# Sample attention of a one-core decoder step: key tiles moved between the compression units, value fills between the later ones, masks applied after the scores

## What is computed

```python
def compress(rows, pe, w1, w2):            # 32-token blocks at stride 16
    ...
    for j in range(n_part):
        pre = pre + u[:, j, j:j + n_blk]
    return jnp.einsum('bngh,hd->bngd', jax.nn.silu(pre), w2)

def cmp_branch(q, q_pos, kc_rows, vc_rows, W):
    kc = rmsnorm(compress(kc_rows, ...), W['k_norm'])
    vc = compress(vc_rows, ...)
    ...
    return attend_shared(q, q_pos, kc, vc, e, mask, W['rel_bias'])   # also gives p_cmp

def select_blocks(p_cmp, q_pos, n_sel, k_top):   # the 16 best blocks of 64 tokens
    imp = jnp.sum(p_cmp, axis=3)
    ...
    _, idx = lax.top_k(score, k_top)
    return idx
```

## Time and profile before

| what | us |
|---|---|
| median of 3 runs | 1774.26 (1773.98 to 1776.72) |
| the profiled execution, its own time | 1760.02 |
| its span, first to last instruction | 1758.2 |
| PE busy in it | 1669.6 (95%) |
| DVE busy | 1148.0 (65%) |
| ACT busy | 762.8 (43%) |
| granted TensorE clock, mean | 0.98 of 2.4 GHz |

### The profile page before, as it was taken

The page is one execution under the profiler, slowest core; times in us unless marked ns, Lnnn a source line. Parts: engine busy times, 40 slices in busy tenths (PEclk is TensorE's granted clock), DMA queues, the critical chain, the costliest instruction groups (busy, mean ns, idle before and its releaser), DMA issues. The chain is left out here.

```text
span 1758.2 us, 32849 instructions
## 1 busy us (share of the span) xinstructions
PE 1669.6 (95%) x11957; PEld 1434.0 (82%) x11957; DVE 1148.0 (65%) x2529; ACT 762.8 (43%) x1585; POOL 432.1 (25%) x548
## 2 busy tenths in 40 slices
PE   5999999799998989998987998999999999999999
PEld 5999999689887666655655877999999999977887
DVE  6632247666766555556464368887778887687885
ACT  6322453677774235456443234322322332365342
POOL 1321110666775543334352001000000000040000
PEclk9999999799999989999998999999999999999999
DMA  5533211120101247547593232322222332593343
GB/s 162 99 107 108 53 43 26 25 50 21 25 16 29 65 143 272 192 142 272 173 398 136 73 97 65 116 91 97 90 90 94 107 112 84 176 381 96 94 120 108
DMA packets 158858, 204.24 MB, mean 116 GB/s; under 512 B 55110, under 2 KB 109423, under 8 KB 158674
## 3 DMA queue, kind: packets, MB, share of 16 engines
q1 hardware_dynamic: 136058, 121.66, 23.2%
q0 software_dynamic: 22368, 80.46, 12.9%
q10 hardware_dynamic: 312, 0.52, 0.1%
HBM read 164.69 MB, written 37.90 MB: 115 GB/s over the span
## 5 line engine op out<-in xcount | busy, mean ns | idle before, releaser
L2977 PE MATMUL banks<-u_sum,w_sum 128*128 128x264 f32 x2904 | 358.4, 285 | 3.4 <-DVE w_sum L3008 3.4
L2977 PEld LDWEIGHTS banks<-u_sum,w_sum 128*128 128x128 f32 x2904 | 355.7, 189 | 4.1 <-DVE w_sum L3008 4.0
L470 PE MATMUL banks<-u_parts_mix,w_in_parts 128*128 128x352 f32 x1440 | 243.5, 326 | 4.4 <-DVE u_parts_mix L838 4.4
L470 PEld LDWEIGHTS banks<-u_parts_mix,w_in_parts 128*128 128x128 f32 x1440 | 230.7, 189 | 7.8 <-DVE u_parts_mix L838 4.8
L1982 PE MATMUL banks<-turned,cmp_w 128*128 128x512 f32 x256 | 133.4, 603 | 4.7 <-DVE turned L2109 3.0
L2107 ACT ACTIVATE turned<-banks 128x512 f32<-128x512 f32 (+1 forms) x136 | 78.7, 587 | 125.8 <-PE banks L1970 125.5
L3316 PE MATMUL banks<-wd_hi,gd_hi 128*128 128x512 f32 x308 | 120.2, 390 | 1.4 <-DVE gd_lo L3347 1.0
L3316 PE MATMUL banks<-wd_lo,gd_hi 128*128 128x512 f32 x308 | 120.0, 390 | 0.0
L3316 PE MATMUL banks<-wd_hi,gd_lo 128*128 128x512 f32 x308 | 119.9, 389 | 0.0
L1970 PEld LDWEIGHTS banks<-consts,rows_grouped 128*128 128x128 f32 x512 | 64.7, 144 | 66.7 <-issue 57.2
L3204 POOL DMA_DIRECT2D rest_whole<-g_rest x1 | 0.6, 594 | 466.3 <-issue 466.3
(11 more groups left out here) (459 smaller groups left out, 3340.1 us busy)
## 6 DMA issues: line engine op xcount, KB each, us to landing
gd_whole<-g_sums SPq DMA_DIRECT2D x77, 256.0 KB, 2.7
g_sums<-silu_gate SPq DMA_DIRECT2D x55, 256.0 KB, 2.1
w_gate_raw<-in_w_gate SPq DMA_DIRECT2D x11, 1024.0 KB, 5.4
w_up_raw<-in_w_up SPq DMA_DIRECT2D x11, 1024.0 KB, 5.4
w<-in_w_down POOLq DMA_DIRECT2D x33, 256.0 KB, 18.4
w_in_raw<-in_w_in SPq DMA_DIRECT2D x29, 256.0 KB, 3.4
g_sums<-s SPq DMA_DIRECT2D x22, 256.0 KB, 2.3
x_tile<-in_x_prompt SPq DMA_DIRECT2D x8, 512.0 KB, 4.1
```

The lines of the kernel that those rows point to most:

```text
L470: mm = nc.tensor.matmul(bank[:, 0:PIECE], w[:, pb, :], u[:, pa, k, tokens(p)], start=(k == 0 and (pa, pb) == TERMS[0]), stop=(k == KT - 1 ...
L2977: mm = nc.tensor.matmul(bank(tg, i), wp[side, p][:, a, k, :], m.u[tg, i, b][:, k, :], start=(k == 0 and (a, b) == TERMS[0]), stop=(k == kh ...
```

## The change

`sample_order` is rewritten. In the first half each of units 0 to 7 is followed by one key tile of half 0, and the window follows tile 7; `kc` of half 0 stands inside unit 8. Then units 9 and 10. The ten value fills of half 0 stand one behind each half of units 11 to 14 (eight), two behind unit 14. Tiles 0 and 1 of half 1 stand inside unit 15, tiles 2 to 4 behind it, then `kc`, tiles 5 to 7, window, values. The mask of half 0 can't be there when its tiles are scored, so all eight tiles of each half are copied raw by ACT, and DVE masks and reduces them later, in four pieces of 1024 columns (`mask_max`), in four steps that follow each other. The scores of half 0 go to banks 6 and 7. `sample_chunks` follows the new order. The queries are placed (16 small copies) after unit 0 instead of unit 3. ACT copies half of each key tile's fills in both halves.

```diff
@@ sample_order
-    for u in range(9):
-        fills += comp(u)
-    fills += comp(9, range(6)) + kc(0) + comp(9, range(6, 8)) + comp(10) + keys(0) + win(0)
-    for u in range(11, 16):
-        fills += comp(u)
-    return fills + weights(0) + keys(1, range(1)) + kc(1) + keys(1, range(1, 8)) + win(1) + weights(1)
+    for m in range(4):
+        fills += comp(2 * m) + keys(0, [2 * m]) + comp(2 * m + 1) + keys(0, [2 * m + 1])
+    fills += win(0) + comp(8, range(2)) + kc(0) + comp(8, range(2, 8)) + comp(9) + comp(10)
+    for i in range(8):
+        fills += comp(11 + i // 2, range(4 * (i % 2), 4 * (i % 2) + 4)) + weights(0)[i:i + 1]
+    fills += weights(0)[8:] + comp(15, range(4)) + keys(1, range(2)) + comp(15, range(4, 8))
+    return fills + keys(1, range(2, 5)) + kc(1) + keys(1, range(5, 8)) + win(1) + weights(1)
@@ sample_chunks
+    for m in range(4):
+        chunks += comp(2 * m) + four("keys", 0, m) + comp(2 * m + 1)
+    chunks += comp(8) + comp(9) + comp(10)
+    for m in range(4):
+        chunks += comp(11 + m, [0]) + four("values", 0, m) + comp(11 + m, [1])
...
@@ the vector engine
-                def mask_first(hb):
-                    dve.wait_ge(s.raw_taken, 4 * hb + 4)
-                    dve.wait_ge(s.masked, hb + 1)
...
+                def mask_max(hb, e):
+                    dve.wait_ge(s.raw_taken, 8 * hb + 2 * e + 2)
+                    dve.wait_ge(s.masked, hb + 1)
+                    half = e // 2
+                    part = w.ss[:, DS + 1024 * e:DS + 1024 * (e + 1)]
+                    if half:
+                        near = part.rearrange("p (s n) -> p s n", s=8)[:, :, 120:128]
...
+                        chain(nc.vector.tensor_tensor(near, near, recent, ALU.add))
+                    v = part.rearrange("p (s j x) -> p s j x", s=8, x=4)
+                    chain(nc.vector.tensor_tensor(
+                        v, v, w.mask[:, 32 * half:32 * half + 32].unsqueeze(1).unsqueeze(3).broadcast_to([P, 8, 32, 4]),
+                        ALU.add))
+                    chain(nc.vector.tensor_reduce(w.pm[:, e:e + 1], part, AX.X, ALU.max))
...
+                        for e in range(4):
+                            if since == ((28, 29, 30, 31), (26, 27, 28, 29))[hb][e]:
+                                mask_max(hb, e)
@@ the scalar engine
-                        for j in range(4):
+                        for j in range(8):
                             if f == at["keys", hb, j, 3] + 2:
                                 raw_scores(hb, j)
-                        for e, later in enumerate(((6, 9, 12, 15), (3, 4, 5, 7))[hb]):
-                            if f == at["keys", hb, 7, 3] + later:
+                        for e, since in enumerate(((32, 33, 34, 35), (30, 31, 32, 34))[hb]):
+                            if f == END[hb] + since:
                                 scores_exp(hb, e)
```

More of the change, by code:

```diff
@@ L1799, in sample_order, with key_bank @@
     fills = []
-    for u in range(9):
-        fills += comp(u)
-    fills += comp(9, range(6)) + kc(0) + comp(9, range(6, 8)) + comp(10) + keys(0) + win(0)
-    for u in range(11, 16):
-        fills += comp(u)
-    return fills + weights(0) + keys(1, range(1)) + kc(1) + keys(1, range(1, 8)) + win(1) + weights(1)
-def sample_chunks():
-    comp = lambda us: [("comp", u, sh, h) for u in us for sh in range(2) for h in range(2)]
-    four = lambda kind, hb: [(kind, hb, h, sh, b) for h in range(2) for sh in range(2) for b in range(B4)]
-    return (comp(range(11)) + four("keys", 0) + comp(range(11, 16)) + four("values", 0) + four("keys", 1) +
-            four("values", 1))
+    for m in range(4):
[5 more added lines that the diff above has]
+    return fills + keys(1, range(2, 5)) + kc(1) + keys(1, range(5, 8)) + win(1) + weights(1)
+def sample_chunks():
+    comp = lambda u, halves=range(2): [("comp", u, sh, h) for sh in halves for h in range(2)]
+    four = lambda kind, hb, m: [(kind, hb, m // 2, m % 2, b) for b in range(B4)]
+    chunks = []
+    for m in range(4):
[3 more added lines that the diff above has]
+        chunks += comp(11 + m, [0]) + four("values", 0, m) + comp(11 + m, [1])
+    chunks += comp(15, [0]) + four("keys", 1, 0) + comp(15, [1])
+    for kind, first in (("keys", 1), ("values", 0)):
+        for m in range(first, 4):
+            chunks += four(kind, 1, m)
+    return chunks
+def key_bank(hb, j):
+    return j % 2 if hb and j >= 2 else 6 + j % 2
 def ring_slot(m, n):
@@ L1851, in by_act @@
         if kind == "keys":
-            return order[f][3] % 2 == 1 or (order[f][2] >= 4 and order[f][3] == 2)
+            return order[f][3] % 2 == 1
         if kind == "comp":
@@ L2022, in score @@
                         copied(pe, f - 3 + b)
-                    if j < 2:
-                        pe.wait_ge(s.added, 2 * (10 + j) if hb == 0 else 32)
-                    elif j < 6:
-                        pe.wait_ge(s.raw_taken, 4 * hb + j - 1)
-                    else:
-                        pe.wait_ge(s.s_taken, 4 * hb + j - 5)
+                    if hb == 0 and j == 0:
+                        pe.wait_ge(s.q_placed, 1)
+                    if hb and j < 2:
+                        pe.wait_ge(s.o_ready, 1)
+                    elif hb and j < 4:
+                        pe.wait_ge(s.added, 32)
+                    elif j >= 2:
+                        pe.wait_ge(s.raw_taken, 8 * hb + j - 1)
                     for b in range(B4):
-                        mm = nc.tensor.matmul(m.bank[(j + 1) % 2][32 * b:32 * b + 32, :], w.q[:, hb, b, :],
+                        mm = nc.tensor.matmul(m.bank[key_bank(hb, j)][32 * b:32 * b + 32, :], w.q[:, hb, b, :],
                                               w.fill[:, (f - 3 + b) % SLOTS, :], start=True, stop=True)
@@ L2054, in weigh @@
                     copied(pe, f)
-                    if hb and i == 0:
-                        pe.wait_ge(s.o_ready, 1)
+                    if i == 0:
+                        if hb:
+                            pe.wait_ge(s.o_ready, 1)
+                        else:
+                            pe.wait_ge(s.w_taken, 1)
                     if i < 8 and i % 2 == 0:
@@ L2089, in _ @@
                         project(LAST[f - 4])
-                    if f - 22 in END:
-                        importance(END.index(f - 22))
+                    for hb in range(2):
+                        if f == END[hb] + (22, 20)[hb]:
+                            importance(hb)
                     turn(f + 3)
@@ L2165, in raw_scores @@
                         weights_turned(act, 7)
[L2166 removed]
+                    nc.scalar.activation(w.ss[:, DS + j * 512:DS + (j + 1) * 512], m.bank[key_bank(hb, j)][:, :],
                                          ACT.Copy).then_inc(s.raw_taken, 1)
@@ L2265, in compressed_max @@
                                             negate=True).then_inc(s.c_ready, 1)
-                    chain(nc.vector.tensor_reduce(w.pm[:, 5:6], w.ss[:, 0:DS], AX.X, ALU.max))
+                    chain(nc.vector.tensor_reduce(w.pm[:, 4:5], w.ss[:, 0:DS], AX.X, ALU.max))
                 def compressed_weights(hb):
@@ L2329, in take_window @@
                         weights_turned(dve, 9)
-                    nc.vector.tensor_copy(w.sw[:, 0:WIN], m.bank[1][:, :]).then_inc(s.w_taken, 1)
+                    nc.vector.tensor_copy(w.sw[:, 0:WIN], m.bank[key_bank(hb, 7)][:, :]).then_inc(s.w_taken, 1)
                     dve.wait_ge(s.w_taken, hb + 1)
```

74 lines of the change are left out of this document (21 added, 53 removed).

## The result

The changed kernel takes 1819.45 us (median of 4 runs, 1817.32 to 1820.69) where the kernel before took 1774.12 beside it: 2.5% slower, ratio 1.0253 (95% interval 1.0235 to 1.027). The forecast was 1815, slower. The profiled execution took 1818.66 us, 58.6 more than the one before was forecast from. Outside the stage nothing moved: 813.6 us follow its last output, 813.8 before. The stage itself ran from 645.5 to 1003.2, 357.7 us instead of 298.9, where some 340 had been forecast.

What follows compares the result with a forecast made beforehand. PE was taken to bound the stage, so only its waits counted: 58.2 us comes, 17.6 goes, +40.6 on the profiled 1760.0. With 14.2 from profile to median that made 1815, range 1797 to 1833.

Steps and rivals of the forecast that it cites:

- (a): Key tiles behind units 0 to 7 and 15: PE waits 1.19 us for a late DVE copy, nine times, 10.7.
- (b): Normalisation ahead of `kc` in both halves: PE waits 5.3 and 4.4 us, 13.3 with two low stretches.
- (f): Query copies, first half's gathers and raw copies come at no cost; gathers 0 to 6 us if slow, 0 taken.
- (c): Half 0's mask pieces in unit 10: waits of 5.1 us, 6.9 with a low stretch, plus 2.0 for exponentials: 8.9.
- (d): Ring of gathers, units 12 to 14: slots free late, wait 3.4 us plus low stretch 1.8, three times: 15.6.
- (e): Half 1's mask pieces behind tile 7: first weights 12.3 us after its score, 7.9 more, 9.7 with a low stretch.
- The 4.17 stays: Second half's values: PE's 4.17 us wait for the last value gathers remains, since they are issued as before.
- Clock: After longer idle times PE runs slowly for a stretch, each costing 1.8 us.
- the 3.63: PE's 3.63 us wait for half 0's last value gathers, forecast to go; a block at full speed, 1.08, followed it.
- PE's lead hides it: Rival: PE turning three fills ahead covers late copies, so (a), (c) and (d) vanish: 1768 us, chance 0.06.
- Slower, and more: Rival: first half's gathers land late, (f) and ring waits at 6 each, regroupings hold tiles' copies: 1830 us, chance 0.13.
- Slower, but less: Rival: the clock doesn't fall after the new waits, or only after some: 1802 us, chance 0.16.

Runs made afterwards that it cites:

- the pair from one chip: Kernel before and changed kernel, both unchanged, run and traced in one set on one chip (kind A): 1775.75 and 1816.75 us.
- e_regroup_early: On top of `e_keys_last`, two regroupings of each unit after a first-half key tile moved ahead of the tile: 1798.49 us, 40.5 above before (kind B).
- e_six: Changed kernel with gathers reordered, normalisation earlier, masks spread, then adds, Silu and projection one step later: 1778.38 us, 3.3 above before (kind A).
- kind B: Sets of runs in which the kernel before takes 1758 us; the one recorded chip is 11.
- kind A: Sets of runs in which the kernel before takes 1774 to 1775 us; the recorded chip is 12.
- e_keys_last: Changed kernel with the second unit's four chunks gathered ahead of the key tiles' four in the first half's pairs: 1806.63 us, 33.1 above before (kind A).
- e_after_again: The changed kernel, unchanged, run again beside the kernel before (kind A): 1816.75 us against 1775.75, ratio 1.0239.
- e_no_mask_add: Changed kernel without the addition of the block mask to the raw scores in both halves: 1786.44 us, 28.4 above before (kind B).

## Why the prediction was right

The median came out 4.5 us above the forecast, inside the range. Its steps, with the sizes in the pair from one chip unless another trace is named:

- **(a)** Nine waits at tiles forecast at 10.7: 10.5 (eight in the first half, one in unit 15). `e_regroup_early` shows that it isn't the regroupings, and in `e_six` moving the two adds by one fill (with Silu and projection) was enough to end seven of them; the shift alone was never moved.
- **(b)** Waits of 5.3 and 4.4 forecast: 5.8 (1.31, 0.88, 3.62) and 3.4 here, 4.45 and 3.42 in kind B. In kind A too it is 4.45 alone where the bursts of gathers are shorter (`e_keys_last`), so 1.4 of the 5.8 belong to (f) and not to the normalisation. The table loads were priced rightly: in `e_regroup_early` one starts at 775.07, as the copy ahead of it ends, and the function behind it at 776.36, 1.29 later.
- **(c)** 5.1 forecast: 1.98 + 2.38 = 4.4; no wait of its own for the exponentials, for which 2.0 had been taken. Without the clock, the term was 2.7 too high.
- **(d)** 3.4 three times: 2.67, 2.70, 2.82. The step that was off is the landing: 4.85 us was taken between the earlier trace rows, and in the trace with the result DVE had the rows 4.06 us after the gather's issue began (853.03 to 857.09). The chain with 4.06 gives 2.6. The Trainium skill, "DMA: Bandwidth & Descriptors", section "Anatomy of one DMA — SWDGE (gpsimd) path", whose fit made an estimated 3.2 here, is about as far below the measured 4.06 as the forecast was above. By it the waits would have come out at 1.7.
- **(e)** First weights 12.3 us after tile 7's score: 13.3 (965.69 to 978.99 in the trace with the result). "The 4.17 stays" holds in kind B only (3.96 to 4.64). In kind A there is no such wait, before the change or after it.
- **Clock.** Low stretches were priced 1.8 each, 9.0 net of those that go. PE's busy time in the stage grew by 6.9 in the pair of kind A (285.0 to 291.9) and by 12.0 in kind B (272.8 to 284.8 in `e_regroup_early`). One wait of 2.70 is followed by a block at full speed (1.12 at 875.2), one of 2.67 by a slow one (1.72 at 856.6). The prediction's own case of a wait without a low clock was misread: behind the 3.63 the first product takes 1.08, but the next one like it, from 880.92, takes 1.94.
- **(f), the first half.** Taken as 0 of "0 to 6". In kind B it is 0. In kind A PE stops 6.1 us (2.08, 1.38, 1.28, 1.39) in `e_after_again` and 7.3 in the trace with the result, and `e_keys_last`, which cuts the bursts, is 9 to 12 us faster. The step that failed is not the landing that it named, but that a burst of gathers would cost the other engines nothing.
- **The rivals.** "PE's lead hides it" is out: a wait of 1.19 stood in nine tiles in spite of the lead. "Slower, and more" needed (f) at 6, which kind A had, and ring waits at 6 with their low stretch, which no trace has (the longest wait is 3.08). "Slower, but less" needed a clock that doesn't fall; it fell.
- **The sum.** 40.6, made on a profile of kind B. There `e_regroup_early`, whose waits are those forecast for the changed kernel, is 40.5 above before, its stage 338.3 us against 297.8. Part of that agreement is luck: the sum had 31.6 of idle time and 9.0 of low clock, and the trace has 28.5 more idle (25.0 to 53.5) and 12.0 more busy, two errors of 3 us that cancel. The changed kernel itself has no run of kind B. In kind A it is 41.7 and 45.3 above. That it would lie 14 us over the profiled sum was luck: the 14 us were taken for a constant of the kernel, and they are the difference between the kinds.

**What makes kind A longer isn't shown.** In the kernel before, 12.2 of its 16 us are busy time of PE: the granted clock from 880 to 920 us is 0.83, in kind B 0.98. Its mark in the waits are late starts of PE, DVE and ACT for which no row names a releaser, at and behind bursts of four and more gathers, in both kernels. In the kernel before most of them lie in half 0's values, which had one wait for a DMA in kind B. Timeline of PE, kind A, then kind B:

```profile
876.65 0.40 PE L1994 MATMUL banks<-cmp_w_both,hidden_s 128*128 128x128 f32 x2 [0.59 <-issue]
...
895.45 0.64 PE L2069 MATMUL banks<-new_v,turned 4*32 4x128 f32 x3 [0.84 <-issue]
```

```profile
879.00 1.08 PE L2069 MATMUL banks<-cache_ring,turned 128*32 128x128 f32 x32 [2.99 <-DMA cache_ring<-in_cache_v_sel,half_rows]
```

The DMA engines are full at the first half's stops (1.01 to 1.07 in four short windows of the changed kernel). But full DMA engines don't stop PE by themselves. Windows at the end of a burst of twelve, the changed kernel in kind A, then `e_no_mask_add`, with the same gathers, in kind B:

```profile
689.00:691.00 2.00, 0.31 (x3) 0.07 (x1) 0.36 (x1) 0.00 (x0) 0.50 (x1) 1.00 1.04 406
```

```profile
688.00:690.00 2.00, 2.00 (x11) 1.18 (x10) 0.98 (x2) 0.71 (x2) 0.94 (x2) 1.00 1.02 414
```

Instructions that arrive late, behind the gathers' packets, would look like this, but that is only a guess: an instruction packet starts at 911.7 in the changed kernel, and PE falters from 912.4 to 917.4. Others of these packets fall beside no stop, and no run moves the one without the other.

## What to carry to other kernels

Interleaving two kinds of work that both lean on a third engine (here DVE) need not hide its work; here it put each handover of one kind in the way of the other (nine waits of about 1.2); count what stands ahead of each copy before counting busy shares. In a ring of buffers with one in-order issuer, order the requests by when they are wanted and by when their slot comes free: one whose slot frees late holds all behind it, which then go out in one burst (here POOL stood 18.6 us for a key tile's slot and then issued twelve). Take profile and median from the same set of runs before a difference between them goes into a sum.

## What was not expected of the hardware

The same program differs by some 14 to 17 us between two kinds of set, steady within each (1756.5 to 1762.7 and 1770.9 to 1780.4), and all of it arises in the one stage of 300 us whose indirect gathers come in bursts; outside it the two agree within 1 us. Most of it is not waiting but a slower PE. And in kind A late starts of PE, DVE and ACT go with the bursts: in the first half's traces 1.2 to 4.4 us behind twelve gathers in a row, 0 to 2.0 behind eight, with the same bytes moved.
